# The two dilated groups of prompt attention in residue-class tiles, merged by a running maximum

## What is computed

```
SWA_GROUPS = ((128, 1), (512, 4), (2048, 16))
def dilated_attend(q, k_src, v_src, q_idx, dil, n_keys):
    idx = q_idx[:, None] - dil * jnp.arange(n_keys)[None, :]
    ok = idx >= 0
    ...
    s = jnp.einsum('bqhd,bqnhd->bqhn', q, kg).astype(jnp.float32) * (HEAD_DIM ** -0.5)
    s = jnp.where(ok[None, :, None, :], s, -jnp.inf)
    m = s.max(-1, keepdims=True)
    p = jnp.exp(s - m)
    den = p.sum(-1, keepdims=True)
    o = jnp.einsum('bqhn,bqnhd->bqhd', (p / den).astype(v_src.dtype), vg)
    return o, (m + jnp.log(den))[..., 0]
...
        wgt = jax.nn.softmax(jnp.stack(lses), axis=0)
        o_b = jnp.einsum('gbqh,gbqhd->bqhd', wgt, jnp.stack(outs).astype(jnp.float32))
```

## Time and profile before

| | us |
|---|---|
| median of 3 runs | 1561.87 (1561.52 to 1563.39) |
| the profiled execution | 1563.41 |
| its span, first to last instruction | 1561.3 |
| first score product of the prompt attention | 182.46 |
| last evacuation of its scale by ACT begins | 252.98 |
| ACT's first copy of turned keys begins | 254.17 |

### The profile page before, as it was taken

The page is one execution under the profiler, slowest core; times in us unless marked ns, Lnnn a source line. Parts: engine busy times, 40 slices in busy tenths (PEclk is TensorE's granted clock), DMA queues, the critical chain, the costliest instruction groups (busy, mean ns, idle before and its releaser), DMA issues.

```text
span 1561.3 us, 24279 instructions
## 1 busy us (share of the span) xinstructions
PE 1479.7 (95%) x9372; PEld 1312.1 (84%) x9372; DVE 909.5 (58%) x1734; ACT 562.7 (36%) x1062; POOL 60.4 (4%) x90
## 2 busy tenths in 40 slices
PE   7999898889999999999999999989899999999995
PEld 6888676679999999778798888768899999998784
DVE  4644354386666666635731877765766666664546
ACT  3222276333333333432323433541333333343231
POOL 1002200010000000000100100110100000000000
PEclk9999999989999999999988999989999999999998
DMA  5235324533233222534412211361122222214211
GB/s 196 88 101 178 114 66 119 168 80 83 81 82 84 82 82 71 203 140 144 138 52 79 81 54 55 113 210 55 55 82 81 81 81 81 81 54 132 82 67 61
DMA packets 153911, 153.56 MB, mean 98 GB/s; under 512 B 12374, under 2 KB 123222, under 8 KB 153382
## 3 DMA queue, kind: packets, MB, share of 16 engines
q1 hardware_dynamic: 149938, 139.54, 29.3%
q0 software_dynamic: 3904, 13.07, 2.4%
HBM read 140.76 MB, written 21.91 MB: 104 GB/s over the span
## 4 chain that ended last, share of the span: by engine, by line
PE 86%; DVE 7%; ACT 3%; issue 2%; DMA 1%; POOL 1%; SPq 0%; ACTq 0%; DVEq 0%; POOLq 0%
PE ps L702 70%; PE ps L713 5%; PE ps L683 4%; PE ps L1069 1%; PE ps L777 1%; PE ps L811 1%; ACT w_hi L1209 1%; DVE x_reg L1796 1%; DVE x_reg L1800 1%; ACT attn_side L1195 1%; DVE w_lo L1583 1%; PE ps L990 1%; POOL w_lo L2186 1%; DVE x_reg L1778 1%; DVE ln_stats L1785 1%
## 5 line engine op out<-in xcount | busy, mean ns | idle before, releaser
L702 PE MATMUL ps<-xh_reg,w_hi 128*128 128x288 f32 x1552 | 465.2, 300 | 8.6 <-DVE xl_reg L1590 5.1
L702 PE MATMUL ps<-xl_reg,w_hi 128*128 128x288 f32 x1552 | 460.8, 297 | 0.0
L702 PE MATMUL ps<-xh_reg,w_lo 128*128 128x288 f32 x1552 | 460.8, 297 | 0.0
L702 PE MATMUL ps<-w_hi,xh_reg 128*128 128x512 f32 x768 | 308.0, 401 | 7.9 <-DVE xl_reg L1837 3.4
L702 PEld LDWEIGHTS ps<-xh_reg,w_hi 128*128 128x128 f32 x1552 | 295.1, 190 | 11.0 <-issue 6.2
L702 PE MATMUL ps<-w_hi,xl_reg 128*128 128x512 f32 x768 | 302.1, 393 | 0.0
L702 PE MATMUL ps<-w_lo,xh_reg 128*128 128x512 f32 x768 | 301.8, 393 | 0.0
L702 PEld LDWEIGHTS ps<-xl_reg,w_hi 128*128 128x128 f32 x1552 | 295.2, 190 | 0.0
L702 PEld LDWEIGHTS ps<-xh_reg,w_lo 128*128 128x128 f32 x1552 | 294.9, 190 | 0.0
L1583 DVE TENSOR_TENSOR w_lo<-raw,w_hi 128x2048 fp32r<-128x2048 f32 (+1 forms) x51 | 111.4, 2184 | 244.1 <-ACT w_hi L1209 244.1
L702 PEld LDWEIGHTS ps<-w_hi,xh_reg 128*128 128x128 f32 x768 | 145.9, 190 | 40.4 <-issue 7.2
(11 more groups left out here) (204 smaller groups left out, 1462.3 us busy)
## 6 DMA issues: line engine op xcount, KB each, us to landing
raw<-in_ffn_w_up SPq DMA_DIRECT2D x88, 512.0 KB, 4.9
raw<-in_ffn_w_down SPq DMA_DIRECT2D x40, 512.0 KB, 4.6
raw<-in_attn_w_in SPq DMA_DIRECT2D x24, 512.0 KB, 4.8
raw<-in_gla_w_in SPq DMA_DIRECT2D x24, 512.0 KB, 4.5
out_swa_s<-in_state_swa_kv SPq DMA_DIRECT2D x16, 496.0 KB, 6.5
x_reg<-in_x_prompt SPq DMA_DIRECT2D x8, 512.0 KB, 7.4
raw<-in_gla_w_out SPq DMA_DIRECT2D x8, 512.0 KB, 4.8
out_swa_p<-arena POOLq DMA_DIRECT2D x18, 128.0 KB, 3.3
```

The source lines that it names most:

```text
L702: mm = pe.matmul(out, lhs(i, a), rhs(i, b), start=first and i == 0 and a + b == 0, stop=last and i == ks - 1 and a == 1)
```

## The change

The prompt attention becomes 16 passes. Eight class passes come first, one for each residue class and pair: groups 2 and 3 of the 128 queries of a class against the 128 keys of the same class, one block per group, with two masks of 128 columns, one maximum and one exponential per half. They leave an unscaled output `o_class`, a maximum and a denominator for each token. These statistics are turned to rows, put in token order and turned back (`stats_to_rows`, `stats_to_cols`). Then eight tile passes do groups 0 and 1 for each query tile and pair. Group 1's maximum is taken over its own scores and the class maximum, the class's share is scaled by the exponential of the difference (`class_exp`), its denominator added (`invert`). Six columns of scales are turned (`turn_scales`) and spread to all rows by three products (`spread_scales`) instead of the diagonals; `scale_out` adds the class output.

So that classes are contiguous, the values of units 10 and 11 are formed with every fourth token as the weights of PE, and ACT's copies of turned queries and keys of groups 2 and 3 write in class order. The stores of those values follow that order. SP waits for the last output before it loads the output projection's weights, since part of their place now holds `o_class`.

```diff
+                if n in CLASS_UNITS:
+                    three_products(ps[:, t, :], lambda i, a: parts[a][:, k0 + i, 0:NP].rearrange("p (j r) -> p r j", r=PQ)[:, t, :],
+                                   lambda i, b: w[b][:, i, :], kn, first, last).then_inc(steps, 1)
+                    return
...
+            def turn_scales(p):
+                q = p - CLASSES
+                pe.wait_ge(inverse_ready, q + 1)
+                turn([(0, rden[:, q % 4, :])])
+
+            def spread_scales(p):
+                pe.wait_ge(turned_out, batch_of("scales", p) + 1)
...
+                for k in range(3):
+                    mm = pe.matmul(ps[:, bank, k * P:(k + 1) * P], spread_of[:, k, :], scale_rows, start=True, stop=True)
+                mm.then_inc(turned, batch.one())
...
+            def stats_to_rows(pair):
+                pe.wait_ge(probs, probs_before(PQ * (pair + 1)))
+                turn([(r * P, class_stat[:, PQ * pair + r, :]) for r in range(PQ)])
...
+            for p in range(len(PASSES)):
+                turn_probs(p, 0)
+                if p and not is_class(p - 1):
+                    spread_scales(p - 1)
+                if p + 1 < len(PASSES):
+                    for e in events(p + 1)[1:]:
+                        scores_of(p + 1, e)
+                turn_probs(p, 1)
+                values(p)
+                if p + 2 < len(PASSES):
+                    scores_of(p + 2, events(p + 2)[0])
+                if not is_class(p):
+                    turn_scales(p)
+                if p in TO_ROWS:
+                    stats_to_rows(TO_ROWS[p])
+                if p in TO_COLS:
+                    stats_to_cols(TO_COLS[p])
+            spread_scales(len(PASSES) - 1)
...
+                        if rc % 2 and rt < PQ:
+                            take(qkT[:, 4 * rc:4 * rc + 4, 0:NP].rearrange("p c (r j) -> p c j r", r=PQ)[:, :, 32 * rt:32 * rt + 32, :],
+                                 lambda b: b.rearrange("p (c j r) -> p c j r", c=4, r=PQ))
+                            continue
...
+            def take_class_out(p):
+                _, r, pair = PASSES[p]
+                act.wait_ge(valued, p + 1)
+                act.activation(o_class[:, pair, :].rearrange("p (j r) -> p r j", r=PQ)[:, r, :], ps[:, (4, 7)[p % 2], 0:P],
+                               ACT.Copy).then_inc(o_classed, 1)
...
+            for p in range(len(PASSES)):
+                take_probs(p, 0)
+                if p and not is_class(p - 1):
+                    take_spread(p - 1)
+                take_probs(p, 1)
+                if p + 1 < len(PASSES):
+                    exps(p + 1, 0)
+                    exps(p + 1, 1)
+                if is_class(p):
+                    take_class_out(p)
+                else:
+                    if not is_class(p - 1):
+                        round_out(p - 1)
+                    take(scale_rows, lambda bank: bank[0:6, 0:P])
...
+            def invert(p):
+                _, at, pair = PASSES[p]
+                q = (p - CLASSES) % 4
+                dve.wait_ge(probs, probs_before(p + 1))
+                dve.tensor_tensor(class_den[:, q, :], tile_stat[:, pair, at, 2:4], class_exp[:, q, :], ALU.mult).then_inc(vec, vs.one())
+                settle()
+                dve.tensor_tensor(den[:, q, 2:4], den[:, q, 2:4], class_den[:, q, :], ALU.add).then_inc(vec, vs.one())
+                settle()
+                dve.reciprocal(rden[:, q, 0:4], den[:, q, :]).then_inc(vec, vs.one())
+                settle()
+                dve.tensor_tensor(rden[:, q, 4:6], class_exp[:, q, :], rden[:, q, 2:4], ALU.mult).then_inc(inverse_ready, 1)
+
+            def scale_out(p):
...
+                dve.tensor_tensor(o_pair, ps[:, (4, 7)[p % 2], 0:256], o_scale[:, 0:256], ALU.mult).then_inc(vec, vs.one())
+                dve.tensor_tensor(o_scale[:, 256:384], o_class[:, pair, qi * P:(qi + 1) * P], o_scale[:, 256:384],
+                                  ALU.mult).then_inc(vec, vs.one())
+                settle()
+                dve.tensor_tensor(o_pair[:, P:2 * P], o_pair[:, P:2 * P], o_scale[:, 256:384], ALU.add).then_inc(o_made, 1)
```

More of the change, by code:

```diff
@@ new lines, in turn_probs, with values @@
+            def turn_probs(p, b):
+                blocks = prob_blocks(p)
+                pe.wait_ge(probs, probs_before(p) + (b + 1 if is_class(p) else 2 * b + 2))
+                for i in range(0, len(blocks), 4):
+                    turn([(j * P, pair_buffer(p)[:, b, col:col + P]) for j, (col, _, _) in enumerate(blocks[i:i + 4])])
+            def values(p):
+                _, _, pair = PASSES[p]
+                blocks = prob_blocks(p)
+                bank = (4, 7)[p % 2]
+                if p >= 2 and is_class(p - 2):
+                    pe.wait_ge(o_classed, p - 1)
+                elif p >= 2:
+                    pe.wait_ge(o_made, p - 2 - CLASSES + 1)
@@ L801, in values @@
                 seen = 0
                 for merged in range(2):
-                    mine = [i for i, blk in enumerate(blocks) if (blk[2] > 0) == bool(merged)]
+                    mine = [i for i, blk in enumerate(blocks) if is_class(p) and merged == 0 or not is_class(p) and blk[2] == merged]
                     for i in mine:
@@ L1670, in first_scores, with take_scores @@
-            def first_scores(n):
-                if n >= 2:
-                    dve.wait_ge(turned, PAIR_BATCH[n - 1])
-                elif n == 1:
+            dve.tensor_copy(class_mask[:, 0:P], masks[:, MASK_AT[0] + 3 * P:MASK_AT[0] + 4 * P]).then_inc(vec, vs.one())
+            dve.tensor_copy(class_mask[:, P:2 * P], masks[:, MASK_AT[2] + 3 * P:MASK_AT[2] + 4 * P]).then_inc(vec, vs.one())
+            settle()
+            def take_scores(p, e):
+                kind, at, _ = PASSES[p]
+                dve.wait_ge(s_ready, e + 1)
+                for b in range(2):
+                    bank, buf = ps[:, 2 * (e % 2) + b, :], pair_scores[(p + 1) % 2][:, b]
+                    if kind == "class":
+                        dve.tensor_tensor_reduce(buf[:, 0:2 * P], bank[:, 0:2 * P], class_mask, 1.0, LOWEST, ALU.add, ALU.max,
+                                                 class_stat[:, p, b:b + 1]).then_inc(s_read, 1)
+                        continue
+                    g = e % 2
+                    full = 256 if g else 512
+                    width = min((at + 1) * P, full)
+                    acc = mx[:, (p - CLASSES) % 4, 2 * g + b:2 * g + b + 1]
+                    dve.tensor_tensor_reduce(buf[:, g * HALF:g * HALF + width], bank[:, 0:width],
+                                             masks[:, MASK_AT[g] + full - width:MASK_AT[g] + full],
+                                             1.0, LOWEST, ALU.add, ALU.max, acc).then_inc(s_read, 1)
```

354 lines of the change are left out of this document (182 added, 172 removed).

## The result

The changed kernel takes 1579.84 us in the median of 4 runs (1578.63 to 1583.29), the kernel before 1561.69 (1559.56 to 1563.39) in the same comparison: a ratio of 1.0119 with a 95% interval of 1.0105 to 1.0133. The prediction was +2 us, its range ended at 1576. The loss is 18.2 us.

The account below looks back on a forecast made before the run. PE was taken to bound the stage, ACT only 9 us behind. Stage 72.7 us against 71.7 (+1.0) and projection +1.0 gave +2.0 us: 1565.4 on the profiled execution, 1564 on the median; range 1559 to 1576.

Parts of the forecast that it names:

- The interval: First score to ACT's first key copy, 71.7 us before; each microsecond won or lost there reaches the end in full.
- The projection: Two value units loading every fourth token as weights: 0.01 us per product, 1.0 us in all.
- The clock: Stage priced at granted clock 1.00; rival: PE's clock falls, tile passes cost 5 to 15 us more, chance 0.08.
- The tail: End of the stage, last pass's scales, spread, output steps and rounding until the key copies: 3.1 us, before 1.2.
- the tile passes: Second half of the stage, eight passes: 6.4, 5.9, 5.3 and 4.2 us by tile, 43.6 us for two pairs.
- The switch: From class to tile passes: first wide scores add 0.6 us, then ordinary tile passes follow.
- the class half: First half of the stage, eight class passes with statistics turned and first wide scores: 24.0 us.
- the class pass: In the class half: first pass 4.3 us, then one every 2.3 us, seven more 16.1 us.
- the copies that write every fourth word: ACT's copies of the two rows of statistics: up to 0.5 us more each, 0.5 taken for both.
- the hops: Gaps from engine to engine over the 16 passes: 1.5 us taken, from about 1.5 to 2.
- the wait behind the spread: In a tile pass, ACT idles 1.1 us after the spread while PE does scores and transposes.
- The rival by which these passes take 5 us longer: Rival: 0.3 us more in each of 16 passes, total 1565.5 to 1570 us, chance 0.17.

Follow-up runs that it names:

- e8: Kernel before with 48 of its 148 transposes and 48 of its 148 value products left out, passes kept; 1546.27 us, 0.9912 of before.
- e12: Changed kernel with only four unneeded products added on PE ahead of the first class pass; 1575.54 us in one run.
- e2: Changed kernel with value-unit weights loaded from neighbouring tokens, class order of those values left out; 1583.26 us.
- e5: Changed kernel with unneeded PE products, fewer than in e1, fitted to the waits; 1570.82 us, 1.0061 of before.
- e1: Changed kernel with unneeded products added on PE at its waits in class passes, tile passes and tail; 1585.84 us, 1.014 of before.
- e3: Changed kernel with unneeded PE products added only in the lead-in and class passes; 1579.90 us in one run.
- e4: Changed kernel with unneeded PE products added only in the tile passes and tail; 1591.12 us in one run.
- e7: Changed kernel with the spread of scales moved behind the next pass's second scores, nothing added; 1571.83 us in one run.
- e14: Changed kernel with e10's two moves, unneeded PE products ahead of the first pass and in late passes, rounding moved to DVE; 1558.13 us, 0.9982 of before.
- e9: Changed kernel with the first scores of the pass after next moved ahead of a pass's values; 1569.90 us in one run.
- e10: Changed kernel with the moves of e9 and e7 together, nothing added; 1567.01 us, 1.0038 of before.

## Why the prediction was wrong

**The interval was right.** The stage got 18.1 us longer and the kernel 18.2 slower, so a microsecond there does reach the end. The same holds downwards in e8 (-13.4 and -14.0); in the other kernels stage and time, measured against before, differ by up to 2.5 us.

**The projection was right.** 1.0 us was put down for strided weight loads; two units now take 0.4 us more each, 0.8 in all. The Trainium skill (Advanced Engine Details and Errata, Memory Cachelines) says that such a pattern pays; the trace agrees, with 293 ns per load against 188, a factor of 1.56, and nearly all of that lies beside the product that runs meanwhile.

**The clock was the step that failed.** The stage was priced at a granted clock of 1.00 on the ground that a stretch with 2.21 busy of 4 us had kept it, and the fall was made a rival with a chance of 0.08. It happened. Its price can be taken from kernels with the same order at 1.00. To the first spread: e12 36.8 against 40.9, so 4.1 us. The next four passes: e2, whose clock was 1.00 in 227 to 255 us, has its first and fifth spread 25.1 us apart, the changed kernel 29.2, so 4.1. The last three passes: 14.0 in e5 (added products included) against 16.1, so at least 2.1. The tail: 2.8 against 3.6. The spreads of e2, and of e5:

```profile
229.21 0.90 PE ps L868 x6
...
254.28 0.90 PE ps L868 x6
```

```profile
248.21 0.90 PE ps L877 x6
...
262.20 0.87 PE ps L877 x6
```

Together about 11 us, for the profiled execution; in e2 the first part alone lost 10. That lies inside the 5 to 15 that the rival was given, in part by luck: the rival saw the price in the tile passes, and some 4 of the 11 us fell before them. The chance was what failed: one quiet stretch that keeps 1.00 says little about a dozen short passes in which PE waits in each. The Trainium skill (TensorE: Matmul & The Clock Gate, Part 1) calls the low clock the default that activity releases; the runs agree as far as they go, since added work that nobody needs kept 1.00 where the clock fell without it (e1, e3, e4, e12).

**The switch was the second step.** At 1.00 the prediction has 24.0 us for the class half and 6.4 for the first tile pass up to its spread, 30.4; e12 shows 36.8. Part of it is the class pass, 2.58 us for 2.3 (seven times 0.28, 2 us), and a little the copies that write every fourth word, 1.07 and 1.09 us where 0.6 each and 0.5 more for both were put down. The rest is the switch: the sum gave the first wide scores 0.6 us and then one ordinary pass, but with short class passes ahead there is nothing of a tile pass under way, and scores, reductions, exponentials and row copy stand one behind another for 7.7 us, in e12 at 1.00 just as in the changed kernel. This is read from the chains; no run shortened the switch. I had counted the filling of the first class pass and forgotten that of the second half.

**The tile passes were nearly right.** At 1.00 e2 shows 6.7, 6.6, 5.9 and 5.8 us between spreads; I had 6.4, 5.9 and 5.3 by tile. With e5's last three that is 39.1 us for seven passes, where the forecast has 37.2 without the hops. That the wait behind the spread is part of them is borne out by e7 (0.4 us a pass when it is removed), that ACT's work is, by e14 in part. The rival by which these passes take 5 us longer is true of the half clock only. The tail, put down as 3.1 us from the last values on (its terms add up to 3.0), is 272.76 - 268.53 = 4.2 in the changed kernel, at half clock; in e5, at 1.00, it is 264.98 - 261.45 = 3.5 with 0.55 of added products in it.

So of the 17 us by which the stage missed its 72.7, some 11 are the clock and some 6 the class half and the switch; the 1.9 us more in the tile passes are about what had been allowed for hops and copies. Working with a full clock the change would have come to about 78.7 us of stage, still 7 longer than before: my forecast of no difference would have failed without the clock as well, though the time would have lain inside the range.

**What stays open.** What exactly makes PE lose its clock. The share of busy time in a stretch doesn't order the cases: e8 kept 1.00 after 2.19 busy of 4 us (183 to 187), e12 after 2.08 (211 to 215), and e3 fell after 2.28. e9 and e10 are the same program through the class half, and their first stretches of 4 us from 183 on read 0.69 and 1.00, the second 0.50 and 0.57: both fell, not at the same moment. So a single trace shows one course of the clock out of several, and the prices above are those of the executions that were profiled.

## What to carry over

Take work off the engine that bounds a stage only after asking what it will wait for in the new shape: here e8 shows the work worth 13 us with the passes kept, and the change as a whole ended 31 us above that. In a chain of short passes look for the products that depend on nothing recent and put them into each wait; that shortened a class pass from 2.58 to 1.9 us, and with four added products ahead of the first pass PE stayed at 2.4 GHz through the class passes. Added work pays only where PE truly waits (e1 held the clock and was slower for it). Look at the clock again in the kernel that wins: e14 still loses it once, at the switch. Count the filling of the chain once for every change of its kind, not once at its start.

## What the runs showed of the hardware

- A short gap has a long shadow: in the changed kernel the clock was 0.51 for 11.5 us behind a stretch of 4.2 us with 2.34 busy, and four extra products of 1.9 us in all in that stretch (e12) kept it at 1.00 for the next 48 us. The second is one execution, but all eight kernels with products there kept 1.00 through the class passes.
- Loads of every fourth fp32 word as weights cost 293 ns instead of 188, and a chained product then comes every 0.235 us instead of 0.227.
- At half clock PE's busy share rises (10.0 of 11.5 us in the changed kernel); work per stretch is read from the counts beside it (60 instructions, against 166 in 26.3 us at 1.00).
